# Sample attention of a hybrid decoder step: keys read transposed, scores and values in four strips of 32 rows, states decayed on ScalarE, two pairs' scores ahead of the state updates

## The reference, cut to what matters

```python
# attention of one sample sequence: 8 queries a head against 256 cached and 8 own keys
sc = einsum('qhd,hkd->hqk', q, concat(cache_k[pages], k_new)) * 64 ** -0.5   # causal on the new keys
o_a = einsum('hqk,hke->qhe', softmax(sc), concat(cache_v[pages], v_new))
# retention of one sample sequence, one chunk of 8 tokens
o = (att * dmat) @ v + (q * dq) @ s
s = s * dc[h] + (k * dk).T @ v          # new state, an output: (8 sequences, 8 heads, 64, 128)
o_r = o * rsqrt(mean(o * o, -1) + EPS) * silu(g)
mixed = concat(o_a, o_r) @ w_out
```

## Time and profile before

| | us |
|---|---|
| median of 3 runs | 1578.92 |
| lowest and highest | 1578.02, 1580.51 |
| the profiled execution's own time | 1581.96 |
| its span in the profile | 1580.2 |
| mixer phase in that span | 208.18 to 299.65 |

### The profile page before, as it was taken

The page is one execution under the profiler, slowest core; times in us unless marked ns, Lnnn a source line. Parts: engine busy times, 40 slices in busy tenths (PEclk is TensorE's granted clock), DMA queues, the critical chain, the costliest instruction groups (busy, mean ns, idle before and its releaser), DMA issues. The chain is left out here.

```text
span 1580.2 us, 25777 instructions
## 1 busy us (share of the span) xinstructions
PE 1246.1 (79%) x11119; PEld 725.0 (46%) x11119; DVE 538.7 (34%) x1312; ACT 217.6 (14%) x463; POOL 171.9 (11%) x146
## 2 busy tenths in 40 slices
PE   6999788796986787986974796896897687677674
PEld 4555466333553453542532666334554353443431
DVE  6216965305234123132122374125234123132122
ACT  2011011201110101010001344011110100110101
POOL 0899711100000000000000300000000000000000
PEclk9999887896898878698687697895899878997986
DMA  6544264483699999999998205832799999999993
GB/s 224 189 171 160 108 203 159 164 340 160 258 428 423 427 426 425 427 426 426 426 427 365 68 2 196 336 127 87 310 423 426 426 426 426 425 427 426 425 425 116
DMA packets 72156, 484.21 MB, mean 306 GB/s; under 512 B 13996, under 2 KB 31916, under 8 KB 46524
## 3 DMA queue, kind: packets, MB, share of 16 engines
q1 hardware_dynamic: 66612, 469.53, 72.5%
q0 software_dynamic: 2976, 11.08, 1.9%
q10 hardware_dynamic: 2448, 1.87, 0.5%
HBM read 466.76 MB, written 15.70 MB: 305 GB/s over the span
## 5 line engine op out<-in xcount | busy, mean ns | idle before, releaser
L1699 PE MATMUL gu<-arena,xgT_e 128*32 128x256 f32 x4096 | 282.2, 429 | 99.4 <-DMA arena<-in_moe_w 97.9
L1699 PEld LDWEIGHTS gu<-arena,xgT_e 128*32 128x32 f32 x4096 | 142.9, 122 | 228.2 <-DMA arena<-in_moe_w 89.4
L1715 PE MATMUL yps<-arena,hidT_e 128*32 128x256 f32 x2048 | 156.7, 458 | 41.1 <-DVE hidT_e L1994 34.9
L1723 PE MATMUL xps<-pick_e,token_rows 128*128 128x128 f32 (+1 forms) x768 | 176.4, 371 | 5.3 <-DVEq L1913 5.3
L1723 PEld LDWEIGHTS xps<-pick_e,token_rows 128*128 128x128 f32 (+1 forms) x768 | 134.3, 238 | 51.9 <-issue 27.7
L1988 DVE TENSOR_TENSOR hid_e<-gu,act_g_e 64x256 f32<-64x256 f32 x64 | 38.3, 599 | 301.6 <-ACT act_g_e L1885 300.3
L661 PE MATMUL z_ps<-win_ring,xT 128*128 128x384 f32 x384 | 132.8, 504 | 0.8 <-PEq L239 0.8
L1715 PEld LDWEIGHTS yps<-arena,hidT_e 128*32 128x32 f32 x2048 | 70.9, 126 | 94.8 <-DVE hidT_e L1994 48.2
L661 PEld LDWEIGHTS z_ps<-win_ring,xT 128*128 128x128 f32 x384 | 74.2, 197 | 52.4 <-issue 8.1
L1998 DVE COPY token_rows<-yps 32x256 f32<-32x256 f32 x64 | 26.6, 415 | 168.1 <-PE yps L1715 168.1
L1707 PE MATMUL hps<-ident,hid_e 32*64 32x32 f32 x1024 | 45.1, 229 | 46.9 <-DVE hid_e L1988 46.9
(11 more groups left out here) (398 smaller groups left out, 1303.8 us busy)
## 6 DMA issues: line engine op xcount, KB each, us to landing
arena<-in_moe_w SPq DMA_DIRECT2D x192, 2048.0 KB, 37.2
win_ring<-in_w_in_even SPq DMA_DIRECT2D x12, 1536.0 KB, 10.4
arena<-in_s_w_glu SPq DMA_DIRECT2D x4, 2048.0 KB, 10.5
arena<-in_w_out_even SPq DMA_DIRECT2D x4, 1536.0 KB, 11.4
scratch_s_cs<-w_cs POOLq DMA_DIRECT2D x8, 576.0 KB, 4.3
arena<-scratch_s_cs SPq DMA_DIRECT2D x1, 4608.0 KB, 36.6
scratch_s_fs<-token_rows POOLq DMA_DIRECT2D x8, 512.0 KB, 3.1
arena<-scratch_s_fs SPq DMA_DIRECT2D x1, 4096.0 KB, 32.3
```

Source lines behind the costliest of these rows:

```text
L1699: last = nc.tensor.matmul(out[STRIP[q], 0:WIDE], x[:, c, :], units[half][:, at:at + WIDE], start=c == 0, stop=c == KC - 1)
L1715: last = nc.tensor.matmul(yps[STRIP[q], 0:WIDE], hidT[:, j, :], w2[:, at:at + WIDE], start=j == 0, stop=j == 3)
L1723: last = nc.tensor.matmul(xps[:].rearrange("p a b -> p (a b)")[:, c * n:(c + 1) * n], xn[0:r, t, c * P:(c + 1) * P], rows_of[0:r, t, 0:n], ...
```

## The change

- **Keys.** `cache_k` is given to the program already transposed, `cache_kT` (pages, 128 features, 4 x 128 tokens), an array laid out on the host beside others that were so before. A page is loaded as before in size and number of DMAs. `keys` and both `keys_copy` go, on PE, ACT and DVE; `pair_scores` reads the pages themselves.
- **Scores.** Rows are now in four strips of 32: strip = 2 j + half holds sequence j and heads 4 half to 4 half + 3. A strip needs two of the four chunks of features. So there are 3 blocks of keys (128, 128, 64) x 2 turns x 4 strips = 24 products of 32 columns of weights, where there were 16 of 64 (8 over 256 keys and 8 over 64).
- **Values.** 3 blocks x 4 strips = 12 products over 256 value columns, where there were 6 over 512. `place` masks and sums 256 columns, 4 heads.
- **States.** ACT multiplies `ss` by its decay in four instructions over all sequences (`decayed_s`); DVE adds each sequence's product in one instruction of 512 columns (`add_state`), with no wait for itself.
- **Squares.** ACT does them, 8 instructions of 128 columns a tile with the sum as by-product, tiles 0 and 1 before the decays, tile 2 after the first Exp.
- **Order.** Pairs are computed in the order in which they are loaded, 0, 2, 1, 3 (`PAIR_ORDER`). PE does `pair_scores(0)`, `pair_scores(1)` ahead of the state updates, and puts `turn_probs(0)`, `values(0)` between them. It no longer waits for `ss_new` 8 ahead of attention.
- **SP.** Pair 3's pages wait for `s_pv` 1 alone; the store of the new states comes behind them and ahead of the `attention_leaves`.

The diff, cut:

```diff
+        PAIR_ORDER = (0, 2, 1, 3)
                     elif m == 3:
-                        sp.wait_ge(S["ss_new"], NSEQ)
-                        sp.dma_start(k.o["ret_sample"][0].rearrange("n h d e -> n (h d) e")
-                                     .rearrange("n (c p) e -> p n c e", p=P), ss[:]).then_inc(S["ss_stored"], 16)
                         sp.wait_ge(S["s_pv"], 1)
...
+                sp.wait_ge(S["ss_new"], NSEQ)
+                sp.dma_start(k.o["ret_sample"][0].rearrange("n h d e -> n (h d) e")
+                             .rearrange("n (c p) e -> p n c e", p=P), ss[:]).then_inc(S["ss_stored"], 16)
+                for i, m in enumerate(PAIR_ORDER):
+                    attention_leaves(i, m)
...
-                    for lo, n_k in ((0, 256), (256, 64)):
-                        for ch in range(4):
-                            for j in range(2):
-                                rhs = kT[:, j, ch, :] if lo == 0 else qt[:, 4 + ch, 256:320]
-                                last = nc.tensor.matmul(ps[NS * j:NS * (j + 1), m % 2, lo:lo + n_k],
-                                                        qb[:, 2 * m + j, ch * 64:(ch + 1) * 64], rhs, start=ch == 0, stop=ch == 3)
+                    for b in range(3):
+                        for turn in range(2):
+                            for strip in range(STRIPS):
+                                j, half = divmod(strip, 2)
+                                ch = 2 * half + turn
+                                rhs = kv(2 * m + j, b, 0)[:, ch * P:(ch + 1) * P] if b < 2 else qt[:, 4 + ch, 256:320]
+                                last = nc.tensor.matmul(ps[STRIP[strip], i % 2, b * P:b * P + (P, P, NS)[b]],
+                                                        qb[:, 2 * m + j, ch * 64 + 32 * half:ch * 64 + 32 * half + 32], rhs,
+                                                        start=turn == 0, stop=turn == 1)
...
-                        for j in range(2):
-                            rhs = kv(2 * m + j, b, 1) if b < 2 else z[0:NS, 2, VA:VA + 512]
-                            last = nc.tensor.matmul(po[NS * j:NS * (j + 1), m % 2, :], prst[0:w, m % 2, b, NS * j:NS * (j + 1)],
-                                                    rhs, start=b == 0, stop=b == 2)
+                        for strip in range(STRIPS):
+                            j, half = divmod(strip, 2)
+                            v = kv(2 * m + j, b, 1) if b < 2 else z[0:NS, 2, VA:VA + 512]
+                            last = nc.tensor.matmul(po[STRIP[strip], i % 2, 0:256], prst[0:w, i % 2, b, STRIP[strip]],
+                                                    v[:, 256 * half:256 * half + 256], start=b == 0, stop=b == 2)
...
+                pair_scores(0)
+                pair_scores(1)
+                pe.wait_ge(S["st_final"], 1)
+                pe.wait_ge(S["kvm"], 1)
+                for n in range(4):
+                    state(n)
+                pe.wait_ge(S["orr"], 3)
+                turn_probs(0)
+                state(4)
+                state(5)
+                values(0)
+                state(6)
+                state(7)
+                turn_probs(1)
+                pair_scores(2)
+                values(1)
+                turn_probs(2)
+                values(2)
+                pair_scores(3)
+                turn_probs(3)
+                values(3)
...
+                act.wait_ge(S["kv_out"], 64)
+                squares(0)
+                squares(1)
+                act.wait_ge(S["states"], 16)
+                act.wait_ge(S["ocross"], 2)
+                for ch in range(4):
+                    nc.scalar.activation(ss[:, :, ch], ss[:, :, ch], ACT.Copy, scale=dc[:, 1, ch:ch + 1]).then_inc(S["decayed_s"], 1)
                 act.wait_ge(S["st_final"], 1)
...
+                probs(0)
+                act.wait_ge(S["squared"], 1)
+                squares(2)
+                probs_copy(0)
+                for i in range(1, PAIRS):
+                    probs(i)
+                    probs_copy(i)
...
+                def add_state(n):
                     dve.wait_ge(S["state"], n + 3)
+                    V.tensor_tensor(ss[:, n].rearrange("p c e -> p (c e)"), pt[:, n % 2], ss[:, n].rearrange("p c e -> p (c e)"), ALU.add
+                                    ).then_inc(S["ss_new"], 1)
...
+                softmax_in(0)
+                dve.wait_ge(S["decayed_s"], 4)
+                for n in range(4):
+                    add_state(n)
+                softmax_in(1)
+                for n in range(4, NSEQ):
+                    add_state(n)
+                place(0)
+                softmax_in(2)
+                place(1)
+                dve.wait_ge(S["squared"], TILES)
+                own.do(V.tensor_scalar(nrm2[:], nrm2[:], 1.0 / DV, EPS, ALU.mult, ALU.add))
+                V.reciprocal(nrm[:], nrm2[:]).then_inc(S["osq"], 1)
+                place(2)
+                softmax_in(3)
+                place(3)
```

217 lines of the change are left out of this document (77 added, 140 removed).

## The result

| | before | changed |
|---|---|---|
| median, us (runs) | 1578.47 (4) | 1555.07 (4) |
| lowest and highest | 1576.60, 1580.51 | 1550.86, 1559.44 |
| the profiled execution's own time | 1581.96 | 1550.86 |
| its span | 1580.2 | 1548.9 |
| mixer phase in that span | 208.18 to 299.65 | 207.10 to 269.71 |

The ratio is 0.9851, with an interval of 0.9821 to 0.9880: faster by 1.2 to 1.8%. The same kernel was run ten more times, in two further comparisons. All 14 times lie between 1546.3 and 1559.4, with a median of 1551.5. The forecast was 1551.7 (1545.5 to 1559.5), and the phase was to end at 272.4, 64.2 after its start. From median to median the time fell by 23.4 here and by 26.5 and 27.7 in the two further comparisons, so the 31.1 between the two profiled executions is more than a typical execution shows.

A forecast was written before the change was run, and what follows sets the result against it. PE was taken to set the mixer phase's pace; summed in order of time, with SP's queue last, the phase ends at 272.4 for 299.65, 27.2 less, giving 1551.7 us from the median; range 1545.5 to 1559.5.

The forecast's parts named there:

- SP's file of leaves: End of mixer phase: small stores behind the 2 MB store, two leaves at 2.1 each, last leaf at 268.5, phase end 272.4.
- the rival with the full clock throughout: Mixer phase with PE never losing the full clock: phase ends at 269.6, gain 30, 1548.9 us; chance 0.17.
- the forecast's for the last pair: Last pair at the lower clock: values(3) takes 2.8, to 266.8, place(3) to 268.0.
- The price list: Mixer phase, full clock: scores 1.3 for 2.35, values 1.45 for 2.87, update 0.98; at 1.2 GHz 2.25, 2.8, 1.70.
- 0.8 of cover, 0.85 forecast: Before the state updates: ACT's decays end at 237.2, DVE needs them at 238.05; PE waits if they come later.
- the cover of 1.1: Before the updates: second pair's pages land by 234.6, scores need them at 235.75; late pages hold updates one for one.
- Here I let the clock fall, as it fell in a stretch of updates.: State updates on PE: full clock for updates 0 to 3, to 241.05, then 1.70 an update for 4 to 7.
- DVE is covered at either clock, and an update stays PE's: State updates: DVE's addition 0.72 with its wait, for 1.12, lies under PE's 0.98 or 1.70 an update.
- Their pages have landed between 257.0 and 258.5: Last pair's pages, 9.2 to 10.7 behind values(0), land before the last scores, which follow values(2) ending at 259.2.
- a sign of being wrong: Named as proving the prediction wrong: PE waiting for decayed_s or pages, small stores waiting over 1.5, or longer next-phase stretches.
- If compute is faster than I have it, SP keeps most of that: End of mixer phase: compute allows 272.0, SP's queue 272.4; SP would keep most of any faster compute.

The follow-up runs named there:

- the keys-only run: The kernel before with keys given transposed and the key transposes and copies gone, all else as before; median 1578.18 us, ratio 1.0001.

## Why the prediction was right, and where it was not

**The total** was right, and the place: 28.9 us out of the mixer phase for 27.2 forecast, with SP's file of leaves as its end. The phase lasted 61.9 to 63.6; the forecast had 64.2 and the rival with the full clock throughout 61.4. The measured phase lies between them. It is the rival's account up to `values(2)`, and the forecast's for the last pair.

**The price list** held. A pair of scores took 1.12 to 1.21 (1.3 forecast), 2.36 at the lower clock (2.25); values 1.56 (1.45), 2.94 at the lower clock (2.8), the 0.1 being the block of new keys, whose 8 records of 64\*32 took 0.64 (0.56 up to the next product) where I had 0.48; an update 0.98; DVE's addition 0.69. No time is lost at the changes of form on PE: updates start at 235.44 behind scores that started at 234.23, with no idle noted. The Trainium skill's page "TensorEngine Tiling (Array Packing)", section "Key Properties", says that a change of tiling mode drains TensorE. In this trace that is worth at most 0.1: scores took 1.12 up to scores of the same form and 1.21 up to an update of another form.

**ACT** did its part, as forecast:

```profile
231.58 1.15 ACT L1101 ACTIVATE ss_state<-ss_state,mixer_dc 128x1024 f32<-128x1024 f32 x1 [1.42 <-PE mix_pd L970]
232.63 3.21 ACT L1101 ACTIVATE ss_state<-ss_state,mixer_dc 128x1024 f32<-128x1024 f32 x3
235.86 1.28 ACT L1084 ACT_TABLE_LOAD   x1
...
236.65 1.50 DVE L1186 TENSOR_TENSOR ss_state<-mix_pt,ss_state 128x512 f32<-128x512 f32 x2 [0.83 <-PE mix_pt L985]
```

A decay takes 1.07 (1.05), and they end at 235.84, while DVE's first addition is released by PE at 236.65: 0.8 of cover, 0.85 forecast. A tile of squares takes 2.4 (2.8). No table load stands around the squares (the one at 235.86 is the Exp's, as before), so no load was added. The Trainium skill's page "ScalarE: Activation LUTs", section "Table sets: the hidden batching unit", says that cheap functions appear in every set; Square is not among those that it names there, and this trace agrees with the sentence for Square beside Exp. The pages of the second pair were in time with all three executions of the changed kernel; with the key pages early and the store on ACT, PE waited 0.59 for them, so the cover of 1.1 was thin.

**The step that failed first: "Here I let the clock fall, as it fell in a stretch of updates."** It did not fall. I had read the earlier trace rows as a stretch of small products at 100% busy in which the clock is lost, and in which PE and DVE do nothing else from 234.3 on. But of the 5 us in which it was lost PE was busy 4.10, and only after the fall, with every product twice as long, was it busy throughout and DVE the one that waited. The rows of the kernel before that I should have looked for are the next one on PE and DVE's up to its first update:

```profile
237.26 10.06 PE L988 MATMUL mix_pt<-z,soft 64*64 64x128 f32 x96 [0.85 <-DVEq L1182]
...
234.77 1.22 DVE L1171 TENSOR_TENSOR token_rows<-mix_po,tmp_o 64x1024 f32<-64x1024 f32 x1 [0.36 <-PE mix_po L978]
236.02 3.66 DVE L1178 SCALAR_TENSOR_TENSOR ss_state<-ss_state,mixer_dc,mix_pt 128x128 f32<-128x128 f32 x12
```

DVE was still adding up the sample rows' retention output until 235.99, and began its first update at 236.02, 0.39 ahead of the end of PE's second one (236.41). Its update with its wait for itself took 1.24, so PE waited 0.85, and then the clock fell. In the keys-only run, which has the same updates, PE waited 0.85 there too and then 0.18, and the clock fell as well (0.79 from 235 to 240). Without decays and without scores ahead DVE began just as late, 0.38 ahead of the end of PE's second update, but its step was 0.69: PE waited 0.36, and the clock stayed. With the decays on DVE and the scores ahead PE waited 0.49, and the clock was lost. So I had set the worth of DVE's cheaper addition at nothing, "DVE is covered at either clock, and an update stays PE's". It is worth 4.6 to 5.5 of phase, for the most part through the clock: by its longer step alone, 0.5 to 1.5 was expected.

**The step that failed second: "Their pages have landed between 257.0 and 258.5", with PE coming to the last scores at 259.2.** The duration was nearly right: 9.2 to 10.7 from the end of `values(0)` was forecast, and from the update behind those values to the last scores it was 11.3 (243.22 to 254.50), in the other two executions 10.5 and 12.0. But with the full clock in the updates PE came to the last scores at 251.9, 2.57 too early for the pages. A faster PE had turned a cover into a wait, and a wait of PE for pages is what the prediction itself had named as a sign of being wrong. The idle time cost the clock (0.82, then 0.50), and with it 1.2 on the last scores, by the prices above. The last values were 1.4 longer too, but that is not the pages' doing: with the key pages early the last scores are back at the full clock, the last values mostly not (1.80 for their first 16 records, 1.93 in the changed kernel), behind waits of 2.08 and 0.66 for the Exp and its copies.

**The two errors had opposite signs**, and SP took up the rest. Compute was done at 264.81, 57.7 after the phase began, where 59.8 was forecast; SP's last leaf made 58.6 of it (265.73), where 60.3 was forecast. So SP's last leaf came 1.7 sooner than forecast and compute 2.1: the clause "If compute is faster than I have it, SP keeps most of that" did not hold here, since the pages and the store behind them had moved ahead too. With the key pages early compute was done 53.5 after the phase began, 4.2 sooner, and the phase gained 2.2, so there SP kept half. That the phase came out within 2.3 of the forecast is luck in part. The chance of 0.17 for the full clock was too low for what was nearly the case.

**What each part is worth**, each undone by itself from a mean of 62.7: order 15.1, decays on ACT 5.5, strips 5.2, squares on ACT 3.1; keys alone, added to the kernel before, 2.3 and nothing measurable in the whole. Each figure rests on one profiled execution. In whole times the order and the decays show (medians of 1564.0 and 1557.4 for 1551.5 of the changed kernel), the strips and the squares are within the scatter. They overlap through the clock, so the sum has no meaning of its own. That the strips are one of the smaller parts, I had not expected.

**What stays open.** Whole times scatter by up to 13 us between executions of one kernel, and the stretch behind the phase by 6 in the profiles (1276.7 to 1282.9, with 1271.6 once); nothing here explains that. Whether it is a number of open requests or the data themselves that make issues stand behind the 2 MB store wasn't tried.

## What to carry to other kernels

When PE and another engine work hand in hand, compare their steps at the full clock, and look when the other engine comes free. If it is late (DVE's first update here, with 1.12 and a wait for itself against PE's 0.98), a wait of PE can cost it the clock (0.85 here, though 1.23 elsewhere did not), and then the trace shows a PE that is busy throughout and a partner that waits, the reverse of the cause; read the row ahead of the fall. Work with no dependence put ahead of such a loop was worth more here than its own length (15.1 of phase for two pairs' scores of 1.1 to 1.2). And where an edit makes an engine faster, recompute every cover that was measured against its old pace, the loads first.

## What the runs showed of the hardware

- The issue of a small DMA right behind a 2 MB store stood 6.2 to 8.2 us in its queue, in nine profiles; behind half of it 3.01. Issued from ACT instead, the store made SP's page issues stand 1.92 and 1.50.
- Products of 64\*64, 16 records (8 products in f32) in 0.96 to 0.98, kept a granted clock of 1.00 for 8 us with one wait of 0.36 among them; waits of PE of 0.49 (with 0.41 of idle time ahead of it), 0.85 and 1.77 among them were each followed by 0.50. A wait of 1.23 between transposes in the kernel before left the clock at 1.00.
- Four products of 32 columns side by side, 128 columns each: 16 f32 products (32 records) in 0.90 to 1.08; the same scores in strips of 64, 32 records too, took 1.80 to 1.97.
- A Copy with a scale on ACT over 1024 columns in 8 pieces of 128 with a stride took 1.07, within 0.1 of the Silu of 1024 contiguous columns.
